# Sums over partitions as rounded part and remainder, placed in other slots of the order

## The reference

```python
h = rmsnorm(x, pre_norm_g[l])
proj = jnp.einsum('btd,dn->btn', h, w_in[l].astype(h.dtype))
q, fz, iv, gate_a, u, ug, gate_b = jnp.split(proj, split_pts, axis=-1)
o_a = hgrn2_mixer(q, fz, iv, lower_bounds[l], hg_norm_g[l]) * jax.nn.silu(gate_a)
o_b = conformer_conv(u, ug, dw_kernel[l], dw_bias[l], conv_ln_g[l], conv_ln_b[l]) \
    * jax.nn.silu(gate_b)
mixed = jnp.concatenate([o_a, o_b], axis=-1)
y = jnp.einsum('btm,md->btd', mixed, w_out[l].astype(mixed.dtype))
x = x + rmsnorm(y, post_norm_g[l])
...
# layernorm, in conformer_conv, over the channels
mu = jnp.mean(xf, axis=-1, keepdims=True)
var = jnp.mean(jnp.square(xf - mu), axis=-1, keepdims=True)
# the norm of a head, in hgrn2_mixer
o = o * lax.rsqrt(jnp.mean(o * o, axis=-1, keepdims=True) + EPS) * norm_g.astype(jnp.float32)
```

## Time and profile before

| what | value |
|---|---|
| median of 3 runs | 864.01 us (863.19 to 864.01) |
| the profiled execution | 860.58 us |
| its span | 858.9 us |
| PE busy | 844.8 us, 98% of the span |
| DVE, ACT, POOL busy | 643.2, 446.7, 402.7 us |
| granted clock, mean | 0.998 of full |

### The profile page before, as it was taken

How to read it: one execution, slowest core, us unless ns; L and a number is a source line. 1 busy time by engine, 2 the same in 40 slices (tenths; PEclk the granted TensorE clock), 3 DMA queues, 4 the chain that set the end, 5 groups by cost and what they waited for, 6 DMA issues and landing times.

```text
span 858.9 us, 12144 instructions
## 1 busy us (share of the span) xinstructions
PE 844.8 (98%) x4162; PEld 708.8 (83%) x4162; DVE 643.2 (75%) x1033; ACT 446.7 (52%) x692; POOL 402.7 (47%) x209
## 2 busy tenths in 40 slices
PE   8999999999999999999999999999999999999996
PEld 7978888888888888888888888888888888888885
DVE  5569779998989994957758486684947893787557
ACT  7853444453432357646647564574656842554442
POOL 3688778799747345242533425244242444032000
PEclk9999999999999999999999999999999999999999
DMA  9989876879405224141331324223231257888945
GB/s 310 257 213 244 224 156 155 196 172 214 123 26 146 80 69 123 50 123 50 98 98 49 98 64 117 63 79 92 62 109 49 77 163 201 225 144 173 270 195 196
DMA packets 127135, 119.15 MB, mean 139 GB/s; under 512 B 3408, under 2 KB 102009, under 8 KB 124537
## 3 DMA queue, kind: packets, MB, share of 16 engines
q1 hardware_dynamic: 117289, 88.24, 33.7%
q0 software_dynamic: 9056, 25.17, 15.9%
q10 hardware_dynamic: 752, 5.25, 1.6%
HBM read 103.96 MB, written 4.19 MB: 126 GB/s over the span
## 4 chain that ended last, share of the span: by engine, by line
PE 95%; ACT 2%; DVE 1%; DMA 1%; issue 0%; DVEq 0%; SPq 0%; ACTq 0%
PE banks L1700 20%; PE banks L1702 19%; PE banks L1701 19%; PE banks L1733 6%; PE banks L1732 6%; PE banks L1734 6%; PE banks L1843 3%; PE banks L1844 3%; PE banks L1845 3%; PE banks L1643 1%; PE banks L1764 1%; PE banks L1754 1%; PE banks L1770 1%; PE banks L1798 1%; PE banks L1773 1%; DVE h_lo L1095 1%
## 5 line engine op out<-in xcount | busy, mean ns | idle before, releaser
L525 POOL TENSOR_TENSOR w_lo<-w_raw,w_hi 128x1024 fp32r<-128x1024 f32 x122 | 309.1, 2541 | 320.7 <-ACT w_hi L659 300.6
L1700 PE MATMUL banks<-h_hi,w_hi 128*128 128x512 f32 x736 | 291.2, 396 | 2.1 <-DVE work L1206 2.1
L1702 PE MATMUL banks<-h_hi,w_lo 128*128 128x512 f32 x736 | 286.7, 390 | 0.0
L1701 PE MATMUL banks<-h_lo,w_hi 128*128 128x512 f32 x736 | 286.5, 389 | 0.0
L1162 DVE SCALAR_TENSOR_TENSOR banks<-work,tap,banks 128x512 f32<-128x512 f32 x238 | 179.8, 755 | 7.9
L1700 PEld LDWEIGHTS banks<-h_hi,w_hi 128*128 128x128 f32 x736 | 138.3, 188 | 30.4 <-DVE work L1206 2.3
L1702 PEld LDWEIGHTS banks<-h_hi,w_lo 128*128 128x128 f32 x736 | 138.1, 188 | 29.2
L659 ACT ACTIVATE w_hi<-w_raw 128x1024 fp32r<-128x1024 f32 x104 | 109.4, 1052 | 100.7 <-PE banks L1702 57.5
L1701 PEld LDWEIGHTS banks<-h_lo,w_hi 128*128 128x128 f32 x736 | 138.3, 188 | 28.0 <-issue 0.5
L1843 PE MATMUL banks<-w_hi,h_hi 128*128 128x512 f32 x128 | 50.8, 397 | 0.0
L1845 PE MATMUL banks<-w_hi,h_lo 128*128 128x512 f32 x128 | 49.9, 390 | 0.0
(11 more groups left out here) (232 smaller groups left out, 1302.1 us busy)
## 6 DMA issues: line engine op xcount, KB each, us to landing
w_raw<-in_w_in SPq DMA_DIRECT2D x112, 512.0 KB, 3.7
w_raw<-in_w_out SPq DMA_DIRECT2D x32, 512.0 KB, 5.3
gates<-in_w_in POOLq DMA_DIRECT2D x12, 512.0 KB, 8.1
work<-in_w_out POOLq DMA_DIRECT2D x12, 512.0 KB, 10.2
work<-h_hi POOLq DMA_DIRECT2D x4, 1024.0 KB, 9.9
work<-h_lo POOLq DMA_DIRECT2D x4, 1024.0 KB, 10.3
mix<-in_x ACTq DMA_DIRECT2D x4, 1024.0 KB, 10.6
out_y<-mix SPq DMA_DIRECT2D x3, 1024.0 KB, 3.9
```

The lines of the kernel that those rows point to most:

```text
L525: g.tensor_tensor(w_lo[:, a], w_raw[:, r * UW:(r + 1) * UW], w_hi[:, a].bitcast(fp32), ALU.subtract).then_inc(lo_done, 1)
L1700: mm(o, wh, hh, start=kt == 0, stop=False)
L1701: mm(o, wh, hl, start=False, stop=False)
L1702: ins = mm(o, wl, hh, start=False, stop=kt == KT - 1)
```

## The change

Each of the three sums is now two matmuls with rounded ones, one of the rounded part and one of the remainder (`column_sums`). ACT makes the rounded part, DVE the remainder, both into the tile `sides`, which is free then. The mean's sum moves behind unit 5 of head 0, the variance's behind slot 2 of head 1, and `ln_rstd` with it from step 1 to step 3. In every head and the last tile, DVE takes the gate's difference behind the near scores and not ahead of them. In the last tile ACT rounds the weights of `out_hi(7)` behind the scale and `mix_hi` and not ahead. The line numbers of the diff's two sides differ.

```diff
@@ -218,6 +218,7 @@
         sides = sb("sides", [P, 2 * SIDES * T], fp32r)
         side_hi = [sides[:, 2 * r * T:(2 * r + 1) * T] for r in range(SIDES)]
         side_lo = [sides[:, (2 * r + 1) * T:(2 * r + 2) * T] for r in range(SIDES)]
+        ysum_parts, vacc_parts, last_sq_parts = zip(side_hi, side_lo)
         y1 = part(12, TT)
         pair_c12 = part(18, 2)
         y0 = gates[:, D:2 * D]
@@ -275,6 +276,7 @@
         (x_scaled3, x_part, x_bias) = sems("x_scaled3 x_part x_bias")
         (mean_done, cen_done, csq_done, vacc_done, var_done, lnr_s) = sems(
             "mean_done cen_done csq_done vacc_done var_done lnr_s")
+        (ysum_hi, ysum_lo, vacc_hi, vacc_lo) = sems("ysum_hi ysum_lo vacc_hi vacc_lo")
         (ln_x, ln_v, ln_s, ln_sig) = sems("ln_x ln_v ln_s ln_sig")
         (gate_taken, gate_s, gate_ls, gate_sig, gate_ready) = sems(
             "gate_taken gate_s gate_ls gate_sig gate_ready")
@@ -921,9 +923,8 @@
                     act.wait_ge(gate_ready, g + 1)
                     act.wait_ge(ln_v, 7 * g + 6)
                     A(t4, OB, ACT.Square).then_inc(osq_done, 1)
-                    if not last:
-                        act.wait_ge(osq_done, 2 * g + 1)
-                        A(sq_hi, t4, ACT.Copy).then_inc(osq_hi, 1)
+                    act.wait_ge(osq_done, 2 * g + 1)
+                    A(last_sq_parts[0] if last else sq_hi, t4, ACT.Copy).then_inc(osq_hi, 1)
                 if u == 7:
                     act.wait_ge(norm_done, g + 1)
                     A(t1, XB, ACT.Ln, scale=1.0 / P, bias=EPSB).then_inc(rs_s, 1)
@@ -937,6 +938,9 @@
 
             for u in range(HEAD_U):
                 head_step(0, u, (N_HEAD - NO_RAW) // RING)
+                if u == 4:
+                    act.wait_ge(ysum_done, J)
+                    A(ysum_parts[0], lnr, ACT.Copy).then_inc(ysum_hi, 1)
                 own(0, u, True)
                 if u >= 6:
                     for j in range(J // 2 * (u - 6), J // 2 * (u - 5)):
@@ -945,9 +949,12 @@
             def head_rest(h, first):
                 for u in range(HEAD_U):
                     head_step(h, u, (N_HEAD - NO_RAW) // RING + 2 * h, squares=h)
-                    if first and u == 1:
+                    if first and u == 3:
                         ln_rstd()
                     late(h - 1, u, first)
+                    if first and u == 0:
+                        act.wait_ge(vacc_done, J)
+                        A(vacc_parts[0], t3, ACT.Copy).then_inc(vacc_hi, 1)
                     own(h, u, False)
                     if u in (4, 5):
                         ln_tile(h - 1, u - 4)
@@ -1016,7 +1023,7 @@
             for at in range(6):
                 mix_hi(at)
             for s in range(OUT_U):
-                if s:
+                if s not in (0, 7):
                     out_hi(s)
                 late(H - 1, s, False, last=True)
                 if s == 0:
@@ -1025,6 +1032,8 @@
                     ln_tile(J - 1, s - 2)
                 for at in {0: (6, 7), 1: (8, 9), 2: (10, 11), 3: (12,), 5: (13, 14), 7: (15,)}.get(s, ()):
                     mix_hi(at)
+                if s == 7:
+                    out_hi(s)
                 if s == 5:
 
                     act.dma_start(gates[:, 0:D], post_norm_g[0].partition_broadcast(P)).then_inc(gain_in, 16)
@@ -1401,9 +1410,6 @@
                                   src[:, 0:HALF].rearrange("p (c g m) -> p c g m", c=TT, m=m)).then_inc(probs_done, 1)
 
             def late(g, u, first, last=False):
-                if u == 1:
-                    dve.wait_ge(gate_s, 3 * (g + 1))
-                    V.scalar_tensor_tensor(t4, sgate, 0.0, t4, ALU.min, ALU.subtract).then_inc(gate_ls, 1)
                 if u == 2:
                     dve.wait_ge(gate_sig, g + 1)
                     V.tensor_tensor(sgate, sgate, t4, ALU.mult).then_inc(gate_ready, 1)
@@ -1418,6 +1424,9 @@
                     for k0, n in {1: ((0, 2), (2, 2)), 2: ((4, 1), (5, 1)), 3: ((6, 3), (9, 3)), 4: ((12, 1),)}[u]:
                         for k in range(k0, k0 + n):
                             take_scores(g, k, LV0 if k0 in (0, 4, 6, 12) else LV1)
+                if u == 1:
+                    dve.wait_ge(gate_s, 3 * (g + 1))
+                    V.scalar_tensor_tensor(t4, sgate, 0.0, t4, ALU.min, ALU.subtract).then_inc(gate_ls, 1)
                 if u == 4:
 
                     dve.wait_ge(st_done, g + 1)
@@ -1429,9 +1438,10 @@
                         dve.wait_ge(st_v, (TT - 1) * g + c)
                         V.scalar_tensor_tensor(state[:, c * P:(c + 1) * P], state[:, (c - 1) * P:c * P], ebl[:, c:c + 1],
                                                XB[:, c * P:(c + 1) * P], ALU.mult, ALU.add).then_inc(st_v, 1)
-                if u == SQ_U and not last:
+                if u == SQ_U:
                     dve.wait_ge(osq_hi, g + 1)
-                    V.tensor_tensor(sq_lo, t4, sq_hi.bitcast(fp32), ALU.subtract).then_inc(osq_done, 1)
+                    hi, lo = last_sq_parts if last else (sq_hi, sq_lo)
+                    V.tensor_tensor(lo, t4, hi.bitcast(fp32), ALU.subtract).then_inc(osq_done, 1)
                 if u == 7:
                     dve.wait_ge(rs_s, 2 * (g + 1))
                     V.tensor_tensor(t1, OB, t1, ALU.mult).then_inc(on_done, 1)
@@ -1445,6 +1455,9 @@
                 if u == 0:
                     v_join("P4", C21, C21, V_JOINED["P6"])
                 own(0, u, True)
+                if u == 3:
+                    dve.wait_ge(ysum_hi, 1)
+                    V.tensor_tensor(ysum_parts[1], lnr, ysum_parts[0].bitcast(fp32), ALU.subtract).then_inc(ysum_lo, 1)
                 if u == 5:
                     centre()
                 if u >= 6:
@@ -1455,6 +1468,9 @@
             def head_rest(h, first):
                 for u in range(HEAD_U):
                     late(h - 1, u, first)
+                    if first and u == 1:
+                        dve.wait_ge(vacc_hi, 1)
+                        V.tensor_tensor(vacc_parts[1], t3, vacc_parts[0].bitcast(fp32), ALU.subtract).then_inc(vacc_lo, 1)
                     if u in (4, 5, 6):
                         ln_tile(h - 1, u - 4, first)
                     own(h, u, False)
@@ -1744,6 +1760,11 @@
                 project(n, n % RING, half, 0 if name == "UG" else 1)
 
 
+            def column_sums(to, parts):
+
+                mm(to, ones_r[:, :], parts[0], start=True, stop=False)
+                return mm(to, ones_r[:, :], parts[1], start=False, stop=True)
+
             def slot(g, u, first, last=False):
                 if u == 0:
                     pe.wait_ge(lev_ready, g + 1)
@@ -1800,13 +1821,8 @@
                             ins = mm(OB[:, v], state[:, (c - 1) * P:c * P], qdec[:, v], start=False, stop=True)
                     ins.then_inc(o_done, 1)
                 if u == SQ_U:
-                    if last:
-                        pe.wait_ge(osq_done, 2 * g + 1)
-                        mm(XB, ones[:, :], t4, start=True, stop=True).then_inc(norm_done, 1)
-                        return
                     pe.wait_ge(osq_done, 2 * (g + 1))
-                    mm(XB, ones_r[:, :], sq_hi, start=True, stop=False)
-                    mm(XB, ones_r[:, :], sq_lo, start=False, stop=True).then_inc(norm_done, 1)
+                    column_sums(XB, last_sq_parts if last else (sq_hi, sq_lo)).then_inc(norm_done, 1)
 
 
             def head(h, first, second):
@@ -1822,12 +1838,12 @@
                     project(N_HEAD + HEAD_U * h + u, u % RING, u % 2, (u // 2) % 2)
                     if not first:
                         slot(h - 1, u, second)
-                    if first and u == 4:
-                        pe.wait_ge(ysum_done, J)
-                        mm(bank(2), ones[:, :], lnr, start=True, stop=True).then_inc(mean_done, 1)
-                    if second and u == 0:
-                        pe.wait_ge(vacc_done, J)
-                        mm(bank(3), ones[:, :], t3, start=True, stop=True).then_inc(var_done, 1)
+                    if first and u == 5:
+                        pe.wait_ge(ysum_lo, 1)
+                        column_sums(bank(2), ysum_parts).then_inc(mean_done, 1)
+                    if second and u == 2:
+                        pe.wait_ge(vacc_lo, 1)
+                        column_sums(bank(3), vacc_parts).then_inc(var_done, 1)
 
             head(0, True, False)
             head(1, False, True)
```

## The result

The changed kernel's median is 863.92 us in 20 runs, that of the kernel before 862.60 us in its 20 (the three runs shown ahead of the prediction were the upper part of these). The ratio is **1.0018, 95% interval 1.0010 to 1.0025**: slower by 0.9 to 2.2 us, clear of noise and and by its middle value, 0.18%, just inside the 0.2% that counts as no change here.

The account below looks back on a forecast made before the run. PE, busy 844.8 of 858.9 us, was taken as the bound. Saved sums of -1.24 us plus head 1's collision of +2.0 gave about +0.8 us; put on the median of 864.01, 864.8 us, range 862.4 to 866.3.

Parts of the forecast that it names:

- rival 3: Collisions both in head 1 and in the last tile's slot 2: +1.5 us, 865.5 us; chance 0.15.
- Part 1, the sums: Three fp32 sums on PE become pairs of 0.45 us, saving 0.42, 0.41 and 0.41, in all 1.24 us.
- Part 2, making the parts: Three new ScalarE copies and three VectorE subtractions are covered by idle time and slack: cost 0.
- Part 3, head 1: Later ln_rstd delays the decays 3.57 us; GpSimd's remainder collides with VectorE's SBUF work; PE stands 2.0 us, bounds 0 to 2.3.
- who is next when both queue: Head 1, GpSimd or VectorE after the scan: GpSimd gives the forecast's +0.8 us, VectorE -0.4 us.
- Part 4, the other heads: Gate's difference behind the near scores in heads 2 to 7: VectorE idles around it, cost 0.
- Part 4, the last tile: Gate's difference held by GpSimd would make PE stand 0.7 us before slot 2; taken as 0, bounds 0 and 0.95.
- rival 4: Slower: PE stands in head 1 and the last tile at both upper ends, +2.0 us, 866.0 us; chance 0.15.
- Part 5, the last tile's end: With out_hi(7) moved, the last h_lo is ready 0.6 us ahead of PE, as before; moved rounding is covered.

Follow-up runs that it names:

- Run 5: Changed kernel with head 1's ln_rstd behind step 4's rounding and last tile's gate difference ahead of near scores, plus variance's pair back in slot 0: ratio 0.9995.
- Run 2: Changed kernel with ACT's weight rounding of step 4 ahead of ln_rstd in head 1, ln_rstd still ahead of the decays: ratio 0.9993 to the kernel before.
- run 3: Changed kernel with the gate's difference ahead of the near scores again in the last tile alone: ratio 1.0013 to the kernel before.
- run 7: Changed kernel with head 1's ln_rstd behind step 4's rounding, last tile's gate difference ahead, and out_hi(7) ahead of the last norm's scale: -1.19 us behind the start.
- run 6: Changed kernel with head 1's ln_rstd behind step 4's rounding and the gate's difference ahead of near scores in all heads: -1.18 us behind the start.

## Why the prediction was right, and where it was off

The forecast was +0.8 us; measured are +1.3 by the trace and +0.9 to +2.2 by the runs. Its main step held, the step on the last tile did not, and what came about is its rival 3 (+1.5), the two collisions together. The prediction had named a wait in slot 2 of the last tile as a sign of being wrong, and that wait is there (0.20 us printed, 0.50 lost). The 0.5 us between forecast and trace are that tile's 0.50, with -0.11 for the sums and +0.13 for head 1, which nearly cancel.

- **Part 1, the sums.** Forecast 1.24 us saved, measured 1.35. A fp32 sum costs 0.90 us and not 0.87: the steps of the matmuls behind it are some hundredths too long as well (0.24 here and there for 0.23), and the prediction took only the difference to the next matmul.
- **Part 2, making the parts.** Forecast 0, measured 0 in the right places. Run 5 prices the cover: 1.24 us if the variance's pair is asked for in slot 0.
- **Part 3, head 1.** Forecast: decays 3.57 us later, GpSimd asked for inside the scans, 2.08 us lost on DVE, PE standing 2.0. Measured, in the prediction's time: decays at 341.06 (3.49 later), GpSimd at 344.74, scans 2.17 us longer, L1444's end at 366.52 where 366.6 was worked out, PE 2.13 us behind. Run 2 shows that the collision did it and not the late logarithm, which fitted as forecast. The prediction's open question, who is next when both queue, went GpSimd's way in both profiles of the changed kernel and in run 3; why it went VectorE's way at 306.25 in the earlier trace rows stays open. The rule of the Trainium skill (SBUF — State Buffer, section "Who interferes with whom"), that a VectorE instruction with two SBUF inputs contends with a GpSimd instruction that reads SBUF, covers the scans as well: 3.54 us with, 1.37 without.
- **Part 4, the other heads.** Forecast 0, measured 0.01.
- **Part 4, the last tile.** This is the step that failed: "I take 0: three orders have to fall as described". I had worked out a stall of 0.7 us and then set it aside. Measured is 0.50. The gate's difference was stopped inside GpSimd's first operation as worked out; the order behind it differed (the product was stopped once more and the level scores ended 0.6 us late, not 0.95). Run 3 shows the cause: with the difference ahead of the near scores the 0.50 is gone. The working deserved more than the 0.15 that rival 3 and the 0.15 that rival 4 had.
- **Part 5, the last tile's end.** Forecast slack 0.6; measured 0.93 (the last h_lo ends at 729.31, PE's last unit is due at 724.80 + 5.44 = 730.24), and no wait. The prediction kept the 4.58 us of the kernel before and overlooked that they held a stop of 0.3 us: with `out_hi(7)` moved, GpSimd's remainder no longer runs beside the scale, which takes 0.75 us and not 1.04.
- **The base.** The absolute forecast of 864.8 us stood on a median of three runs that was 1.4 us above the median of twenty. The change was forecast 0.5 us too small and the base was 1.4 us too high; that the two errors take from each other is luck. On 862.60 the same working gives 863.4 and a range of 861.0 to 864.9, and the measured 863.92 lies in that one too.

## What to carry to other kernels

When an instruction that only has to be done some time later is put ahead of a chain on an in-order engine, ask first what the chain's last link releases on other engines, and beside what that will then run: here `ln_rstd`, 1.2 us of work that could not start until 2.2 us past the decays' old start, since PE's sum was not ready, moved a weight remainder of GpSimd by 3.5 us, from beside VectorE's reads of PSUM to beside its work in SBUF. The repair in head 1 was not to undo the change but to put the same instruction one step further on, into ACT's idle time: -0.84 us where +1.3 had been. With the gate's difference put back in the last tile it was -1.35. With an engine 98% busy, list for each thing it waits for how early that is ready, before making the engine faster.

## What the runs showed of the hardware

- A printed wait of PE cost the program 0.3 us more than its length in all three cases here: 1.82 printed and 2.13 lost (head 1), 0.92 and 1.24 (run 5), 0.20 and 0.50 (the last tile). Half of it is the record of the matmul ahead, which covers the start of the wait, and half slower steps behind it.
- A result that comes 0.1 us ahead of PE or less costs something too, with no wait printed: 0.15 us at 0.1 us of slack (run 7), 0.07 at 0.12 and 0.06 at about 0 (run 6).
- Four scans of 128 columns, both inputs in SBUF, were stopped by a GpSimd subtraction as an elementwise operation is: 1.37 us alone, 3.54 beside it, and the GpSimd operation isn't slowed (2.36 us).
- The same program repeated PE's times at the places followed here to 0.01 us from 60 us on, while its first 60 us differed by 1.7 us between two profiles of the kernel before and by 1.95 between two of the changed one. The granted clock of the first 60 us was 1.00 and 0.97 of full in the first two, and 0.94 in the longest start (+3.4 us); it is not all of it, since the start of run 7 was 1.1 us late with 1.00. Differences between single profiles are to be read behind the start.
